# Gated branch products of a hybrid attention layer as seven half-size products each, and one expert's weights issued earlier

## The chip, the cores and the metric

One core of one Trainium2 chip. The metric is the device time of one execution, in microseconds (us); lower is better. All arithmetic of the part that is changed is float32.

## The reference, cut to what matters

One layer works on 256 tokens of width 1024. An input projection feeds two branches, differential attention (`y_a`) and a gated delta net (`y_b`), each 512 wide. They are merged by two gates, and a mixture of 32 experts follows:

```python
merged = (jax.nn.sigmoid(m_gate_a) * (y_a @ w_branch_attn[layer])
          + jax.nn.sigmoid(m_gate_b) * (y_b @ w_branch_gdn[layer]))
x = x + merged @ w_out[layer]
h2 = rms_norm(x, norm_ffn_gain[layer])
x = x + hier_moe(h2, ...)          # 32 experts, 1024 -> 256 -> 1024, two of them chosen per token
return rms_norm(x, norm_final_gain)
```

The change is in the two products `y @ w_branch`, each (256 x 512) by (512 x 1024).

## The kernel before

Five engine programs run side by side and meet at semaphores: `sync_program` issues nearly all transfers in one fixed order, `gpsimd_program`, `scalar_program`, `tensor_program` and `vector_program` compute. Work is laid out transposed: features on the 128 partitions, 256 tokens in the free direction.

**Stages.** The input projection is cut into 11 chunks of columns (`CHUNKS`, so `NCH` = 11) whose weights (2 MB each) alternate between two staging tiles, `stage0` and `stage1`. The last four chunks (`ma0`, `ma1`, `mb0`, `mb1`, the gates) are already computed with seven products of half size (`products`, L1022, matmul at L1046): GpSimd forms the four sums of weight quarters `S1`, `S2`, `S4`, `S3` (`combine` in `gpsimd_program`, L542, four instructions of 128x256 a form), ScalarE copies products `P1`, `P5`, `P6`, `P4` out of PSUM (L673), VectorE adds `P2`, `P3`, `P7` (L1892 to L1902), and ScalarE takes the sigmoid (L679). Then come the branch products (L1280 to L1301, matmul L1299): weights `w_branch_gdn` in `stage1`, `w_branch_attn` in `stage0`, four pieces `n` of 16 matmuls, each 128x128 weights on 256 token columns, written to a pair of PSUM banks. VectorE multiplies each piece with its gate (L2068) and adds the two branches to `merged` (L2071). Then `mix` (L1315) multiplies `merged` with `w_out`, whose halves use `stage1` and `stage0` again; `logits` (L1324), norms and routing follow, and then the loop over 32 experts (L1451 gate and up, L1494 down).

**A matmul of float32 counts twice** in the profile: the 64 matmuls of the branch products are 128 PE rows, and so on.

**What orders the transfers.** `sync_program` runs down one list and waits where a tile is not free. `stage_free(i)` (L335) waits until the stage tile of chunk `i` has been used. An expert's weights are three transfers of 1 MB (`load_expert`, L360 to L371), in eight slots. Slot 3 is the part of the arena from `A` to `EwT`; the gate and up weights of slot 7 lie in the tile `extra`, which holds the attention's exponentials before; slots 4 and 5 are `dv` to `vn` and `stage1`, slot 6 is `stage0`. Expert 5 waits for half of the mixing, expert 6 for all of it (`mix_out`, L366, L368). Later loads (L437, L442) wait until an expert has been used. The order around the change is: `w_branch_gdn` (L400), `w_branch_attn` (L400), expert 2, first half of `w_out` (L407), expert 3 and gate and up of slot 7, second half of `w_out`, experts 4, 5, 6.

Of the kernel before, what the change touches and what calls it, by code (L numbers as in the profile page):

```python
# [18 lines left out]
ALU = mybir.AluOpType  # L19
# [3 lines left out]
P = 128  # L23
# [5 lines left out]
H = 4  # L29
# [42 lines left out]
COPIED = ("P1", "P5", "P6", "P4")  # L72
ADDED = ("C11", "C12", "C2")
# [6 lines left out]
BANKS = {"ma0": (2, 0, 3, 1), "ma1": (0, 3, 2, 1), "mb0": (3, 2, 0, 1), "mb1": (1, 2, 0, 3)}  # L80
# [52 lines left out]
def lay_out(nc, ctx):  # L133
# [20 lines left out]
    def at(name, size, extra=0):  # L154
        return arena[:, names[name] + extra:names[name] + extra + size]
# [10 lines left out]
    def v3(ap, a):  # L166
        return ap.rearrange("p (a b) -> p a b", a=a)
# [55 lines left out]

    c.x1T = v3(at("qT", 2048), KD)
# [78 lines left out]
    def sem(name):  # L303
# [182 lines left out]
def gpsimd_program(pool, c, io):  # L486
# [96 lines left out]
def scalar_program(act, c, io):  # L583
# [347 lines left out]
def tensor_program(pe, c, io):  # L931
# [348 lines left out]
    for n in range(4):  # L1280
        j, half = n // 2, n % 2
        i = NCH + j
        w = c.stage[i % 2][:, 0:4096].rearrange("p (k n) -> p k n", k=H)
        yT = (c.ybT, c.yaT)[j]
        if n == 1:
            pe.wait_ge(s["ya_ready"], 1)
            turn("yaT", lambda i: c.oa[:, i % 2, (i // 2) * P:(i // 2 + 1) * P])
        pe.wait_ge(s[f"stage_loaded{i % 2}"], 16 * (i // 2 + 1))
        pe.wait_ge(s["ybT_ready" if j == 0 else "yaT_ready"], 1)
        if n == 0:  # L1290
            pe.wait_ge(s["product_copied"], copied("mb1", "P4"))
            pe.wait_ge(s["quarter_added"], added("mb1", "C11"))
        elif n == 1:
            pe.wait_ge(s["quarter_added"], added("mb1", "C2"))
        else:
            pe.wait_ge(s["branch_used"], n - 1)
# [4 lines left out]
        last.then_inc(s["branch_ready"], 1)  # L1301
# [356 lines left out]
def vector_program(v, c, io):  # L1658
# [745 lines left out]
```

## Time and profile before

| | us |
|---|---|
| median of 3 runs (453.85 to 455.72) | 455.1 |
| the profiled execution, its own time | 452.95 |
| its span, first to last instruction | 451.2 |
| PE busy | 422.8 (94%) |
| VectorE busy | 216.1 (48%) |
| ScalarE busy | 124.6 (28%) |
| GpSimd busy | 60.1 (13%) |
| moved by DMA | 136.92 MB, mean 303 GB/s |

Engines: PE is TensorE's matmuls, PEld its weight loads, DVE VectorE, ACT ScalarE, POOL GpSimd; SPq, PEq and so on are the sequencers that issue. The time of the profiled execution is 1.75 us more than its span. A busy share is a mean over stages that have different limits, so it doesn't tell what sets the time of a stage.

### The profile page before, as it was taken

Reading aid. Unit: us, or ns where it says so; the run is one execution under the profiler, and the core shown is the slowest. Engines: PE = TensorE matmul, PEld = TensorE weight load, DVE = VectorE, ACT = ScalarE, POOL = GpSimd, SP = SyncE. Lnnn points to the kernel's source line nnn. Section 1 sums busy time; section 2 is a strip of 40 time slices with the busy share of each in tenths; the row PEclk is TensorE's granted clock in tenths of the full one; section 3 lists DMA queues with packets and bytes.
Section 4 is the critical chain, followed back from the end, with each engine's and each line's share of the span. In section 5 each row is a group of like instructions: output and inputs, shape, how many; then the busy total and the mean of one; then the engine's idle time right before and its main releaser. Section 6 shows DMA issues by size and latency. Waiting matters only on the chain.

```text
span 451.2 us, 10749 instructions
## 1 busy us (share of the span) xinstructions
PE 422.8 (94%) x4503; PEld 337.8 (75%) x4503; DVE 216.1 (48%) x573; ACT 124.6 (28%) x326; POOL 60.1 (13%) x94
## 2 busy tenths in 40 slices
PE   9999999999999999999999899999999986779674
PEld 8885598884899999988889677777686755547351
DVE  3376777896446478022322654444453612433124
ACT  6001622100410455200012533233242411222144
POOL 4010600000558956000000000000000000000001
PEclk9999999999999999999999899999999998899899
DMA  8979826234805045389995999999999999999993
GB/s 308 409 243 302 288 80 214 96 120 100 321 2 188 16 171 187 125 348 410 404 421 201 380 390 425 414 422 420 422 425 418 420 426 420 421 424 421 420 398 118
DMA packets 38197, 136.92 MB, mean 303 GB/s; under 512 B 8592, under 2 KB 9936, under 8 KB 26256
## 3 DMA queue, kind: packets, MB, share of 16 engines
q1 hardware_dynamic: 33808, 135.22, 76.0%
q10 hardware_dynamic: 4352, 1.21, 1.2%
q8 instruction: 23, 0.38, 0.3%
q14 instruction: 14, 0.11, 0.1%
HBM read 134.59 MB, written 1.84 MB: 302 GB/s over the span
## 4 chain that ended last, share of the span: by engine, by line
PE 77%; DMA 18%; DVE 2%; ACT 1%; issue 1%; SPq 1%; POOLq 0%; ACTq 0%; DVEq 0%
PE ps L1000 22%; DMA arena<-in_moe_w_up 12%; PE ps L1046 11%; PE ps L1451 10%; PE ps L1315 6%; PE ps L1299 6%; DMA ring<-in_moe_w_up 6%; PE ps L1494 3%; PE ps L1504 3%; PE ps L1410 3%; PE ps L1459 1%; PE ps L1061 1%; PE ps L948 1%; PE ps L1399 1%; SPq L437 1%
## 5 line engine op out<-in xcount | busy, mean ns | idle before, releaser
L1000 PE MATMUL ps<-arena 128*128 128x256 f32 (+1 forms) x384 | 98.6, 416 | 0.0
L1000 PEld LDWEIGHTS ps<-arena 128*128 128x128 f32 x384 | 72.2, 190 | 22.3 <-issue 13.8
L1451 PE MATMUL ps<-arena 128*32 128x128 f32 x1040 | 38.3, 284 | 11.1 <-DMA arena<-in_moe_w_up 9.2
L1451 PEld LDWEIGHTS ps<-arena 128*32 128x32 f32 x1040 | 29.7, 110 | 17.8 <-DMA arena<-in_moe_w_up 8.4
L797 ACT ACTIVATE gains<-ps 32x256 f32<-32x256 f32 x62 | 23.4, 377 | 54.7 <-PE ps L1494 54.3
L563 POOL TENSOR_SCALAR ring<-ring,small 128x512 f32<-128x512 f32 x1 | 1.6, 1570 | 266.7 <-DVE small L2152 266.7
L2198 DVE TENSOR_TENSOR masks<-ps,masks 128x64 f32<-128x64 f32 x32 | 7.2, 224 | 54.8 <-ACT masks L778 54.6
L542 POOL TENSOR_TENSOR ring<-arena 128x256 f32<-128x256 f32 x32 | 22.7, 741 | 78.2 <-DMA arena<-in_w_in 65.7
L2214 DVE COPY arena<-ps 32x256 f32<-32x256 f32 x62 | 25.8, 416 | 11.4 <-PE ps L1494 10.5
L1451 PE MATMUL ps<-ring,arena 128*32 128x128 f32 x768 | 27.7, 285 | 3.3 <-DMA ring<-in_moe_w_up 3.3
L1315 PE MATMUL ps<-arena 128*128 128x256 f32 x128 | 29.3, 383 | 0.0
L1299 PE MATMUL ps<-arena 128*128 128x256 f32 x128 | 28.0, 379 | 0.0
L1410 PE MATMUL ps<-masks,arena 128*128 128x128 f32 x224 | 27.4, 281 | 0.0
L1451 PEld LDWEIGHTS ps<-ring,arena 128*32 128x32 f32 x768 | 22.1, 112 | 7.1 <-issue 4.0
L1410 PEld LDWEIGHTS ps<-masks,arena 128*128 128x128 f32 x224 | 26.0, 195 | 1.6 <-issue 1.6
L1299 PEld LDWEIGHTS ps<-arena 128*128 128x128 f32 x128 | 24.2, 190 | 3.2
L1315 PEld LDWEIGHTS ps<-arena 128*128 128x128 f32 x128 | 23.9, 190 | 3.0
L1046 PE MATMUL ps<-ring 128*128 128x128 f32 x192 | 23.1, 276 | 0.0
L1046 PEld LDWEIGHTS ps<-ring 128*128 128x128 f32 x192 | 22.1, 192 | 0.1
L1494 PE MATMUL ps<-arena,masks 128*32 128x256 f32 x304 | 20.1, 382 | 0.4 <-DMA arena<-in_moe_w_down 0.4
L739 ACT ACTIVATE arena<-arena 128x256 f32<-128x256 f32 x8 | 3.3, 416 | 46.0 <-DVE arena L2083 46.0
L784 ACT ACTIVATE masks<-ps 64x64 f32<-64x64 f32 x32 | 7.0, 217 | 32.6 <-PE ps L1459 32.6
(323 smaller groups left out, 606.5 us busy)
## 6 DMA issues: line engine op xcount, KB each, us to landing
arena<-in_moe_w_down SPq DMA_DIRECT2D x19, 1024.0 KB, 26.4
arena<-in_w_in SPq DMA_DIRECT2D x8, 2048.0 KB, 8.5
arena<-in_moe_w_gate SPq DMA_DIRECT2D x16, 1024.0 KB, 22.5
arena<-in_moe_w_up SPq DMA_DIRECT2D x16, 1024.0 KB, 23.5
ring<-in_moe_w_gate SPq DMA_DIRECT2D x12, 1024.0 KB, 20.1
ring<-in_moe_w_up SPq DMA_DIRECT2D x12, 1024.0 KB, 20.4
ring<-in_moe_w_down SPq DMA_DIRECT2D x12, 1024.0 KB, 21.7
arena<-in_w_out SPq DMA_DIRECT2D x2, 2048.0 KB, 10.4
```

The source lines that it names most:

```text
L542: pool.tensor_tensor(form[out][:, k, :], one[:, k, :], other[:, k, :], op).then_inc(s["forms_combined"], 1)
L797: last = act.activation(stacked(c, i, q), down_out(c, i, q), ACT.Copy)
L1000: last = pe.matmul(out, lhs, rhs, start=(k == 0 and (i > 0 or part % 2 == 0)), stop=(k == KD - 1), skip_group_check=(i == 0))
L1046: last = pe.matmul(out[:, a, :], forms[held][:, k, a * P:(a + 1) * P], forms[streamed][:, k, :], start=(begins and a == 0 and k == 0), sto ...
L1299: last = pe.matmul(blk(branch_out(c, half), b, TOK), w[:, k, (4 * half + b) * P:(4 * half + b + 1) * P], yT[:, k, :], start=(k == 0), stop ...
L1315: last = pe.matmul(mix_out(c, b), w[:, k, (b % 4) * P:(b % 4 + 1) * P], c.merged[k // 4][:, (k % 4) * TOK:(k % 4 + 1) * TOK], start=(k == ...
L1410: last = pe.matmul(gather_out(c, k), c.h2[:, t, k, :], c.oh[:, t, :], start=(t == 0), stop=(t == NT - 1))
L1451: last = pe.matmul(c.ps[ROWS * q:ROWS * (q + 1), i % 2, 0:P], c.Hg[:, k, ROWS * i:ROWS * (i + 1)], w[:, :, start:start + 127:2], start=(k ...
L1494: last = pe.matmul(down_out(c, i, q), c.actT[i % 2][:, kk * ROWS:(kk + 1) * ROWS], c.down_w[slot][:, kk, 256 * q:256 * (q + 1)], start=(kk ...
L1504: last = pe.matmul(y_out(c, half, t), c.S_e[:, t * P:(t + 1) * P], c.Y[half], start=False, stop=False, skip_group_check=True)
L2198: v.tensor_tensor(sg, bank[:, 0:64], sg, ALU.mult).then_inc(s["gated"], 1)
L2214: last = v.tensor_copy(stacked(c, i, q), down_out(c, i, q))
```

## The change

Each branch product is cut into quarters and computed as seven products of 8 matmuls with 128 token columns. GpSimd forms four sums of weight quarters a branch, VectorE four differences of `y` quarters (`form_branch`), ScalarE copies four products out (`copy_branch`), and VectorE adds the other three and applies the gates in smaller pieces. The transposition of `y_a` (`turn("yaT")`) is now in the middle of the first branch. On the list of transfers, expert 3 moves ahead of `w_branch_attn`, and gate and up of slot 7 move behind expert 4. The two halves of `w_out` wait for the seventh and the fourteenth product. Three blocks of `mix` instead of two are computed in halves before the first `logits`. `FORMS`, `BANK_OF` and `ORDER` are those of the gates.

```diff
+BRANCHES = ("b0", "b1")
+ALL_SEVEN = SEVEN + BRANCHES
-BANKS = {"ma0": (2, 0, 3, 1), "ma1": (0, 3, 2, 1), "mb0": (3, 2, 0, 1), "mb1": (1, 2, 0, 3)}
+BANKS = {"ma0": (2, 0, 3, 1), "ma1": (0, 3, 2, 1), "mb0": (3, 2, 0, 1), "mb1": (1, 2, 0, 3), "b0": (3, 2, 0, 1), "b1": (1, 2, 0, 3)}
...
+    c.branch_sum = {n: v3(at(place_, 1024), 2) for n, place_ in zip(COMBINED, ("dv", "cq", "kdec", "vn"))}
+    c.branch_form = [{n: v3(at("hT", TOK, 1024 * j + TOK * i), 2) for i, n in enumerate(("T1", "T3", "T2", "T4"))} for j in range(2)]
...
+    c.branch_part = [c.extra[:, 2048 * j:2048 * j + 2048].rearrange("p (a f) -> p a f", a=KD) for j in range(2)]
...
-            sp.wait_ge(s["branch_ready"], 2 * (i - NCH - 1))
+            sp.wait_ge(s["branch_ready"], len(ORDER) * (i - NCH - 1))
...
+        if j == 1:
+            sp.wait_ge(s["ybT_ready"], 1)
+            sp.wait_ge(s["ya_ready"], 1)
+            load_expert(3)
         stage_free(i)
         sp.dma_start(c.stage[i % 2][:, 0:4096].rearrange("p (k n) -> p k n", k=H),
...
-        if j == 0:
-            sp.wait_ge(s["ybT_ready"], 1)
-            sp.wait_ge(s["ya_ready"], 1)
-            load_expert(3)
-            load_expert(SLOTS - 1)
     sp.wait_ge(s["yaT_ready"], 1)
     sp.wait_ge(s["side_ready"], len(SIDE))
     sp.wait_ge(s["merged_ready"], 2)
     load_expert(4)
+    load_expert(SLOTS - 1)
...
+    for j, name in enumerate(BRANCHES):
+        i = NCH + j
+        w = branch_quarters(c, j)
+        def free(product):
+            if j:
+                pool.wait_ge(s["branch_ready"], branch_done(0, product))
+        def combine(out, one, other, op):
+            for k in range(2):
+                for f in range(2):
+                    cols = slice(TOK * f, TOK * f + TOK)
+                    pool.tensor_tensor(c.branch_sum[out][:, k, cols], one[:, k, cols], other[:, k, cols], op).then_inc(s["forms_combined"], 1)
+        pool.wait_ge(s[f"stage_loaded{i % 2}"], 16 * (i // 2 + 1))
...
+        free("P5")
+        combine("S1", w["A21"], w["A22"], ALU.add)
...
+        free("P6")
+        combine("S2", c.branch_sum["S1"], w["A11"], ALU.subtract)
...
+        free("P3")
+        combine("S4", w["A12"], c.branch_sum["S2"], ALU.subtract)
+        free("P7")
+        combine("S3", w["A11"], w["A21"], ALU.subtract)
...
+    copy_branch(0, "P1", "C11")
+    copy_branch(0, "P5", "C22")
+    copy_branch(0, "P6", "C12")
     act.wait_ge(s["side_ready"], SI["yaT"] + 1)
     act.activation(c.flat["qT"], c.side[side_pair("yaT")], ACT.Copy).then_inc(s["yaT_ready"], 1)
+    copy_branch(0, "P4", "C21")
...
-        for b in range(4):
-            for k in range(H):
-                last = pe.matmul(blk(branch_out(c, half), b, TOK), w[:, k, (4 * half + b) * P:(4 * half + b + 1) * P], yT[:, k, :],
-                                 start=(k == 0), stop=(k == H - 1))
...
+            out = branch_out(c, j, product)
+            for a in range(4):
+                for k in range(2):
+                    last = pe.matmul(out[:, a, :], forms[held][:, k, a * P:(a + 1) * P], forms[streamed][:, k, :],
+                                     start=(begins and a == 0 and k == 0), stop=(k == 1), skip_group_check=True)
+            last.then_inc(s["branch_ready"], 1)
+    branch_products(0, "P1", "P2", "P5", "P6")
+    pe.wait_ge(s["ya_ready"], 1)
+    turn("yaT", lambda i: c.oa[:, i % 2, (i // 2) * P:(i // 2 + 1) * P])
+    branch_products(0, "P4", "P3", "P7")
+    branch_products(1, "P1", "P2", "P5", "P6", "P4", "P3", "P7")
...
-        for b in range(2):
+        for b in range(3):
             mix(b, ks)
     logits(0)
-    for b in range(2, KD):
+    logits(1)
+    for b in range(3, KD):
...
-    for q in range(4):
-        v.wait_ge(s["branch_ready"], q + 1)
-        v.tensor_tensor(c.branch_gate[q], c.branch_gate[q], branch_out(c, q % 2), ALU.mult).then_inc(s["branch_used"], 1)
-        if q >= 2:
-            v.wait_ge(s["branch_used"], q + 1)
-            v.tensor_tensor(c.merged[q - 2], c.branch_gate[q - 2], c.branch_gate[q], ALU.add).then_inc(s["merged_ready"], 1)
+    form_branch(0)
+    add_branch(0, "C11", "P2", "P1")
+    add_branch(0, "C12", "P3", "P6")
...
+    chain(v.tensor_tensor(g0, g0, flat_half(0, 0), ALU.mult))
+    form_branch(1)
...
+    v.tensor_tensor(low, low, both_tokens(0), ALU.add).then_inc(s["quarter_added"], 1)
...
+    chain(v.tensor_tensor(g1, g1, flat_half(0, 1), ALU.mult))
+    add_branch(1, "C11", "P2", "P1")
...
+    chain(v.tensor_tensor(tokens(g2, 0), tokens(g2, 0), branch_part(c, 1, "C11"), ALU.mult))
...
+    chain(v.tensor_tensor(tokens(g2, 0), tokens(g2, 0), tokens(g0, 0), ALU.add))
+    v.wait_ge(s["product_copied"], copied("b1", "P6"))
+    early = branch_part(c, 1, "C12")
+    chain(v.tensor_tensor(early, early, tokens(g2, 1), ALU.mult))
...
+    chain(v.tensor_tensor(early, early, tokens(g0, 1), ALU.add))
+    v.wait_ge(s["product_copied"], copied("b1", "P4"))
+    low = flat_half(1, 1)
+    chain(v.tensor_tensor(low, low, g3, ALU.mult))
+    v.wait_ge(s["branch_ready"], branch_done(1, "P3"))
+    v.tensor_tensor(tokens(g2, 1), tokens(g2, 1), branch_out(c, 1, "P3"), ALU.mult).then_inc(s["quarter_added"], 1)
...
+    v.tensor_tensor(tokens(g2, 1), tokens(g2, 1), early, ALU.add).then_inc(s["merged_ready"], 1)
+    chain(v.tensor_tensor(low, low, g1, ALU.add))
...
+    v.tensor_tensor(gate3, gate3, both_tokens(1), ALU.mult).then_inc(s["quarter_added"], 1)
...
+    v.tensor_tensor(c.merged[1], low, g3, ALU.add).then_inc(s["merged_ready"], 1)
```

## Rows read from the trace of the kernel before

**Rows 1.** The chain that ended last, in order: start us, us, what

```profile
177.51 8.93 PE ps L1046 x80
186.44 6.91 PE ps L1299 x32
193.35 0.87 PE ps L1054 x8
194.22 20.72 PE ps L1299 x96
214.94 6.91 PE ps L1315 x32
...
335.74 26.11 DMA arena<-in_moe_w_up
```

**Rows 2.** Windows of busy time; the last three columns are PEclk, DMA share, GB/s

```profile
179.00:182.00 3.00, 3.00 (x29) 3.00 (x28) 1.03 (x4) 0.77 (x2) 0.00 (x0) 1.00 0.00 0
182.00:188.00 6.00, 6.00 (x48) 5.80 (x48) 1.11 (x2) 2.47 (x3) 0.00 (x0) 1.00 0.08 20
188.00:201.00 13.00, 13.00 (x66) 11.50 (x65) 1.22 (x1) 1.28 (x2) 0.00 (x0) 1.00 0.97 394
...
203.00:241.00 38.00, 38.00 (x188) 33.71 (x187) 9.89 (x25) 2.50 (x6) 0.00 (x0) 1.00 1.02 411
241.00:246.00 5.00, 5.00 (x31) 4.56 (x30) 1.27 (x3) 2.16 (x4) 0.00 (x0) 1.00 0.04 15
...
332.00:440.00 108.00, 88.94 (x1485) 62.40 (x1487) 37.00 (x114) 29.50 (x102) 0.00 (x0) 0.95 1.01 419
```

**Rows 3.** Timeline, SyncE's issues: start us, us, engine, line

```profile
171.30 0.37 SPq L400 DMA_DIRECT2D arena<-in_w_branch_gdn  x1
...
186.47 0.37 SPq L400 DMA_DIRECT2D arena<-in_w_branch_attn  x1
...
201.16 0.38 SPq L407 DMA_DIRECT2D arena<-in_w_out  x1
...
229.68 0.33 SPq L371 DMA_DIRECT2D arena<-in_moe_w_gate  x1
...
245.28 0.33 SPq L371 DMA_DIRECT2D arena<-in_moe_w_gate  x1
```

**Rows 4.** L400, the two branch weights: from issue to landing

```profile
DMA to landing us min/median/max: 7.7/7.8/7.9
```

**Rows 5.** Timeline around the start of the branch products

```profile
184.49 1.95 PE L1046 MATMUL ps<-ring 128*128 128x128 f32 x16
184.69 0.42 DVE L1896 TENSOR_TENSOR arena<-arena,ps 128x256 f32<-128x256 f32 x1 [4.66 <-PE ps L1046]
186.28 7.07 PE L1299 MATMUL ps<-arena 128*128 128x256 f32 x32
186.48 0.69 DVE L1902 TENSOR_TENSOR arena<-arena,ps 128x512 f32<-128x512 f32 x1 [1.36 <-PE ps L1046]
187.20 1.06 ACT L679 ACTIVATE arena<-arena 128x1024 f32<-128x1024 f32 x1 [2.61 <-DVE arena L1902]
...
214.78 7.07 PE L1315 MATMUL ps<-arena 128*128 128x256 f32 x32
```

**Rows 6.** Groups by line and shape: busy us, mean ns; one ScalarE copy of 128x512

```profile
L2088 DVE TENSOR_TENSOR arena<-arena 128x256 f32<-128x256 f32 x6 | 2.6, 426 | 2.9 <-ACT arena L739 2.9
L2071 DVE TENSOR_TENSOR arena<-arena 128x1024 f32<-128x1024 f32 x2 | 2.5, 1225 | 0.1
...
443.40 0.60 ACT L833 ACTIVATE ring<-ps 128x512 f32<-128x512 f32 x1 [0.17 <-PE ps L1480]
```

**Rows 7.** Timeline of GpSimd's sums, three forms in a row

```profile
136.88 2.79 POOL L542 TENSOR_TENSOR ring<-arena 128x256 f32<-128x256 f32 x4 [7.08 <-DVE extra L1929]
139.74 2.80 POOL L542 TENSOR_TENSOR ring<-ring,arena 128x256 f32<-128x256 f32 x4
142.62 2.79 POOL L542 TENSOR_TENSOR ring<-arena,ring 128x256 f32<-128x256 f32 x4
```

**Rows 8.** Single instructions of VectorE and GpSimd where both read SBUF

```profile
127.80 0.73 DVE L1998 TENSOR_TENSOR arena<-arena 128x512 f32<-128x512 f32 x1 [0.26 <-DVE arena L1994]
127.94 1.17 POOL L542 TENSOR_TENSOR ring<-arena 128x256 f32<-128x256 f32 x1
...
169.12 0.35 DVE L2046 SCALAR_TENSOR_TENSOR arena<-arena,small 128x128 f32<-128x128 f32 x1 [0.16 <-DVE arena L1937]
169.27 0.79 POOL L542 TENSOR_TENSOR ring<-ring,arena 128x256 f32<-128x256 f32 x1
169.39 0.81 DVE L2046 SCALAR_TENSOR_TENSOR arena<-arena,small 128x128 f32<-128x128 f32 x1
```

**Rows 9.** L2057 and L542 by line: ns min/median/max, first and last start

```profile
L2057 DVE SCALAR_TENSOR_TENSOR arena<-arena,small,gains x8: 336/339/915, 177.3 to 179.7; 128x128 f32<-128x128 f32 x8
...
L542 POOL TENSOR_TENSOR ring<-arena x32: 718/727/1172, 118.1 to 177.3; 128x256 f32<-128x256 f32 x32
```

**Rows 10.** Windows around TensorE's pause after the mixing, columns as before

```profile
248.00:250.00 2.00, 1.09 (x9) 0.79 (x7) 1.79 (x13) 2.00 (x2) 0.00 (x0) 1.00 1.03 434
...
252.00:254.00 2.00, 2.00 (x18) 0.65 (x17) 1.30 (x8) 0.00 (x0) 0.00 (x0) 0.50 1.04 438
```

More of the change, by code:

```diff
@@ L117, in copied, with branch_done, branch_formed @@
 def copied(name, product):
-    return len(COPIED) * SEVEN.index(name) + COPIED.index(product) + 1
+    return len(COPIED) * ALL_SEVEN.index(name) + COPIED.index(product) + 1
 def added(name, quarter):
-    return len(ADDED) * SEVEN.index(name) + ADDED.index(quarter) + 1
+    return len(ADDED) * ALL_SEVEN.index(name) + ADDED.index(quarter) + 1
 def combined(name, form):
-    return 4 + 4 * (len(COMBINED) * SEVEN.index(name) + COMBINED.index(form) + 1)
+    return 4 + 4 * (len(COMBINED) * ALL_SEVEN.index(name) + COMBINED.index(form) + 1)
+def branch_done(j, product):
+    return len(ORDER) * j + ORDER.index(product) + 1
+def branch_formed(j, form):
+    return 4 * j + ("T1", "T3", "T2", "T4").index(form) + 1
 class Core:
@@ L221, in lay_out @@
             c.form[f"B{i + 1}{j + 1}"] = c.hT[:, 4 * i:4 * i + 4, P * j:P * j + P]
+    c.branch_sum = {n: v3(at(place_, 1024), 2) for n, place_ in zip(COMBINED, ("dv", "cq", "kdec", "vn"))}
+    c.branch_form = [{n: v3(at("hT", TOK, 1024 * j + TOK * i), 2) for i, n in enumerate(("T1", "T3", "T2", "T4"))} for j in range(2)]
+    for j, yT in enumerate((c.ybT, c.yaT)):
+        for i in range(2):
+            for t in range(2):
+                c.branch_form[j][f"B{i + 1}{t + 1}"] = yT[:, 2 * i:2 * i + 2, P * t:P * t + P]
+    c.branch_part = [c.extra[:, 2048 * j:2048 * j + 2048].rearrange("p (a f) -> p a f", a=KD) for j in range(2)]
     c.x1T = v3(at("qT", 2048), KD)
@@ L569, in weight_quarters, with branch_quarters, branch_part, branch_out @@
     return {f"A{a + 1}{j + 1}": w[:, 4 * j:4 * j + 4, TOK * a:TOK * a + TOK] for a in range(2) for j in range(2)}
+def branch_quarters(c, j):
+    w = c.stage[(NCH + j) % 2][:, 0:4096].rearrange("p (k n) -> p k n", k=H)
+    return {f"A{a + 1}{k + 1}": w[:, 2 * k:2 * k + 2, 512 * a:512 * a + 512] for a in range(2) for k in range(2)}
+def branch_part(c, j, quarter):
+    a, t = int(quarter[1]) - 1, int(quarter[2]) - 1
+    return c.branch_part[j][:, 4 * a:4 * a + 4, P * t:P * t + P]
+def branch_out(c, j, product):
+    return c.ps[:, BANKS[BRANCHES[j]][BANK_OF[product]], :].rearrange("p (a f) -> p a f", a=4)
 def quarters(c, name):
@@ L1277, in tensor_program, with branch_free @@
     products("mb1", "P5", "P6", "P4", "P3", "P7")
-    for n in range(4):
-        j, half = n // 2, n % 2
-        i = NCH + j
[L1283 to L1287, printed above, removed]
+    def branch_free(name, product):
+        prev = ALL_SEVEN[ALL_SEVEN.index(name) - 1]
+        bank, was = BANKS[name][BANK_OF[product]], BANKS[prev]
+        if bank == was[3]:
+            pe.wait_ge(s["product_copied"], copied(prev, "P4"))
+        else:
+            pe.wait_ge(s["quarter_added"], added(prev, ("C2", "C11", "C12")[was.index(bank)]))
@@ L1288, in tensor_program, with branch_products @@
+    def branch_products(j, *wanted):
+        name = BRANCHES[j]
+        i = NCH + j
+        forms = dict(c.branch_form[j], **branch_quarters(c, j), **c.branch_sum)
         pe.wait_ge(s[f"stage_loaded{i % 2}"], 16 * (i // 2 + 1))
         pe.wait_ge(s["ybT_ready" if j == 0 else "yaT_ready"], 1)
[L1290 to L1296, printed above, removed]
@@ L1297, in tensor_program @@
-        for b in range(4):
-            for k in range(H):
-                last = pe.matmul(blk(branch_out(c, half), b, TOK), w[:, k, (4 * half + b) * P:(4 * half + b + 1) * P], yT[:, k, :],
-                                 start=(k == 0), stop=(k == H - 1))
-        last.then_inc(s["branch_ready"], 1)
+        for product in wanted:
+            held, streamed = FORMS[product]
+            begins = product in ("P1", "P2", "P5", "P4")
+            if begins:
+                branch_free(name, product)
+            if product == "P6":
+                pe.wait_ge(s["product_copied"], copied(name, "P1"))
+            elif product == "P3":
+                pe.wait_ge(s["product_copied"], copied(name, "P5"))
+            elif product == "P7":
+                pe.wait_ge(s["product_copied"], copied(name, "P6"))
+            if held in COMBINED:
+                pe.wait_ge(s["forms_combined"], combined(name, held))
+            if streamed[0] == "T":
+                pe.wait_ge(s["branch_forms"], branch_formed(j, streamed))
+            out = branch_out(c, j, product)
[4 more added lines that the diff above has]
+            last.then_inc(s["branch_ready"], 1)
@@ new lines, in both_tokens, with tokens, flat_half, add_branch @@
+    def both_tokens(j):
+        return branch_out(c, j, "P7").rearrange("p a (j f) -> p a j f", j=1).to_broadcast([P, 4, 2, P])
+    def tokens(flat, t):
+        return flat.rearrange("p (a f) -> p a f", a=4)[:, :, P * t:P * t + P]
+    def flat_half(j, half):
+        return c.extra[:, 2048 * j + 1024 * half:2048 * j + 1024 * half + 1024]
+    def add_branch(j, quarter, product, copy):
+        part = branch_part(c, j, quarter)
+        v.wait_ge(s["branch_ready"], branch_done(j, product))
+        v.wait_ge(s["product_copied"], copied(BRANCHES[j], copy))
+        v.tensor_tensor(part, part, branch_out(c, j, product), ALU.add).then_inc(s["quarter_added"], 1)
```

41 lines of the change are left out of this document (38 added, 3 removed).

## The prediction

> **What bounds the kernel now.** I read four views, in this order. First the chain that ended last [rows 1]. Up to some 332 us it is TensorE's own work without a gap: the gate products (L1046), the branch products (L1299), `mix` (L1315). From 335.74 us it is transfers of expert weights, 26 us at a time. The reader is to see that the end is set by DMA, and the stage with the change by TensorE. Second, the windows [rows 2]: from 332 to 440 us DMA is busy all the time at 419 GB/s. So a gain on TensorE counts only if it lets the last stretch of transfers start earlier. Third, that is the question of where DMA has run dry: it moves nothing from 179 to 182 us, next to nothing until 188, and 15 GB/s from 241 to 246. That second gap ends with the issue of expert 6 at 245.28 us [rows 3], which waits for the last block of `mix`, since its slot is `stage0`. What is moved after it has a fixed size. So the end moves with the end of `mix`, us for us, as long as DMA runs dry before it. Fourth, the timeline and the durations of single instructions give the prices [rows 5 to 9].
>
> **TensorE.** Before, from the first branch matmul at 186.28 to the first of `mix` at 214.78 us it takes 28.50 us [rows 5]: 128 rows of 256 columns and the transposition of 0.87 (6.91 + 20.72 = 27.63 for 128, 0.216 each [rows 1]). After, there are 14 products of 8 matmuls, which is 224 rows of 128 columns. That shape is L1046: 80 rows take 8.93 us, so 0.1116 each, 1.786 a product [rows 1]. 14 x 1.786 = 25.0; 27.6 - 25.0 = 2.6 us less. A seventh less arithmetic is 12.5% of 27.6 = 3.4; the shorter rows give 0.8 of it back. If nothing waits, `mix` starts at 212.2 instead of 214.8. `mix` has as many matmuls as before; that three blocks are begun in halves instead of two gives 5.2 us (24 rows of 0.216) instead of 3.5 until `merged[1]` is needed.
>
> **The transfers.** Expert 3 is issued when `ya_ready` comes, with the last L2057 at 180.0 us [rows 9], into the gap of DMA. 3.15 MB at 419 GB/s are 7.5 us, with the 1.9 us that pass between an issue at 186.47 and DMA's first data at about 188.4 [rows 2, 3]: 182.0 to 189.5. `w_branch_attn` is issued at 186.4 as before (it waits for `mb1`) and has 1.1 us of expert 3 ahead of it. Before, it landed 7.7 us after its issue, at 194.2 [rows 3, 4]; now I take 195.3. Behind it go expert 2, until 202, then `w_out`'s first half, issued after the seventh product at 199.7 instead of 201.16, until 207; `mix` wants it at 212. Then DMA is idle until `w_out`'s second half at 212.3 (before 214.97), which is wanted 14 us later. Expert 4 and slot 7 follow: 7.35 MB with it, 17.5 us, until 232. Expert 5 and expert 6 wait for `mix`, 229.68 and 245.28 before [rows 3]: expert 5 is issued near 227 and ends near 239, and expert 6 can't go before 242.7. DMA runs dry again, for 3 to 5 us, so this part gives and costs nothing by itself. The moved loads are paid for by idle time on both sides.
>
> **ScalarE** gets eight copies of 128x512, 0.60 each [rows 6]. It is free after the last sigmoid (187.20 + 1.06 [rows 5]). Each copy begins 0.2 after its product (as L1896 does in rows 5) and is wanted a whole product later, so it hides behind TensorE; without that cover each would cost 0.8.
>
> **GpSimd** gets 32 sums, four a form, 2.86 a form from start to start, 11.4 a branch [rows 7]. Branch 0: 179.3 (weights issued at 171.3 [rows 3], landed 7.9 later [rows 4]) to 190.6. TensorE wants the forms at 189.9, 191.6, 196.1 and 197.9, and they are there at 182.2, 185.0, 187.9 and 190.6. Branch 1: 195.3 to 206.7, wanted at 203.1, 204.9, 208.5 (`P3`) and 210.3 (`P7`), there at 198.2, 201.0, 203.9 and 206.7. 3.5 us of cover, so nothing, if GpSimd works at this pace.
>
> **VectorE is where it gets tight.** `mix` wants `merged[0]`, and its last inputs are late. Undisturbed, from rows 5 and 6 (0.43 for 256 columns, 0.68 for 512, 1.22 for 1024, 0.03 between): add `P3` of branch 0 at 198.0, gate 1.22, four forms 1.7, add `P7` 1.22, gate 1.22, add `P2` 0.68, multiply and add 1.36: at 206.5 it is done and waits for the copy of `P6` (207.6). Two instructions to 209.0, it waits for the copy of `P4` (209.4), multiplies 1024 columns to 210.6, then `P3`'s part and the last add: `merged[0]` at 212.0. TensorE comes at 212.2. No stall, but no slack either, and 1.6 us of waiting on VectorE's side. `merged[1]` comes at 215.8 and is wanted at 217.4.
>
> **But the two engines block each other.** The DVE instruction at 169.39 took 0.81 instead of 0.34 behind a GpSimd sum begun at 169.27, and the slowest L2057 took 0.915 against a median of 0.339; the GpSimd sum begun at 127.94, just after a DVE instruction with both inputs in SBUF, took 1.17 instead of 0.73 [rows 8, 9]. The one begun at 169.12 lost nothing. So a VectorE instruction with two SBUF inputs that meets GpSimd's sums pays 0, 0.47 or 0.58; I take 0.35 as a mean. In branch 1 eight such instructions fall between 198.7 and 209: the gate, four forms, the two with `g2`'s first tokens, the first with `early` (the second gate mostly meets a change of form). 8 x 0.35 = 2.8, less the 1.6 of waiting: `merged[0]` at 213.2 to 213.3. TensorE then stalls 1.2 before `mix`. GpSimd in turn loses 0.18 to a form, 0.45 to 512 columns [rows 8], and about 1.0 (0.45 and the 0.53 that 512 columns more take) to the gate: some 3 us, its last form at 209.5 to 210, wanted at 210.3. `merged[1]`: 217.0, wanted at 218.5.
>
> Beside the rows stands the Trainium skill, SBUF — State Buffer, section "Who interferes with whom": a VectorE instruction with two SBUF inputs and a GpSimd instruction that reads SBUF take an exclusive lock on a shared port, one waits for the other. The trace agrees in kind. The page holds the lock for the whole instruction; by that each meeting would cost up to 0.7, `merged[0]` would come near 215 and the gain would be nil. In rows 8 a sum gives way about 0.2 before its end, so I keep the rows' price.
>
> **The sum.** -2.6 (TensorE) + 1.3 (stall before `mix`, from `merged[0]` at 213.3 and 0.1 to TensorE, less rounding) = -1.3 us. The profiled execution would go from 452.95 to 451.65 us (span 451.2 to 449.9). It was 2.15 below the median of the runs shown, so on that median: 455.1 - 1.3 = 453.8 us. Bounds: the stall 0 (gain 2.6) to 2.9 (loss 0.3), if all eight pay 0.58.
>
> **The rivals.**
>
> *No blocking that matters (chance 0.25).* The meetings fall into gaps, as the first of 169.12 did. Then 2.6 less: 452.5. For it: only four meetings stand in rows 8 and 9, and 1.6 us of slack takes up the first four or five. Against: in branch 1 GpSimd has no pause.
>
> *VectorE pays in full (0.12).* Eight meetings of 0.5 to 0.58, gain between 0.4 and -0.3: 455.
>
> *GpSimd's sums late (0.13), the case on the slower side.* If `w_branch_attn` lands later, because expert 3 stands before it or shares with it, every form is late, and forms that are late meet more of VectorE's work. Up to a landing at 196 the chain above holds. From there on TensorE waits at `P5` to `P7`, and the waits of both engines add. Landing at 197, the last form would be 1.7 later than 209.8, at 211.5, and the two instructions with `early` and part of the next then meet it too (0.45, 0.45 and some 0.5): 212.9, 2.6 after it is wanted, and the gain is gone. Every us beyond costs a us and its share of such meetings, 1.5 together: at 198.5 it is slower by 2.3, 457.4. For it: expert 3 is 3.15 MB in front of a load that has 4 us of slack. Against: 1.1 us is all that is left of it at the issue, and landing times of rows 4 differ by 0.2.
>
> *The earlier load pays by itself (0.03).* 6.3 us of idle DMA from 182 to 188 are filled. If DMA didn't run dry before expert 6, the end would come up to 6 earlier: 449. Against it: 15 GB/s from 241 to 246 [rows 2].
>
> *The clock falls (0.05).* After TensorE's pause at 248 to 250 (1.09 of 2 us busy) the granted clock is 0.50 at 252 to 254 [rows 10], the lower level of 1.2 GHz. If the stall of 1.2 us did that to 4 us of `mix`, 2 us would be added: 455.8. Against: in rows 2 the clock stays at 1.00 everywhere up to 246.
>
> **How the numbers follow.** Forecast 0.42, the rivals 0.25, 0.12, 0.13, 0.03, 0.05. The likeliest time is 453.8, its own range 453.0 to 454.6. The bound of what a measurement can tell, 0.5%, is 2.3 us. Rival one, 2.6, lies just beyond and is measured as faster about half the time, and so is a tail of the forecast: faster 0.13 + 0.07 + 0.03 + 0.02 = 0.25. Slower is the late landing beyond 198 and half of the clock's case, with a tail: 0.13. Same 0.62. The range from 452.0 to 456.2 holds the forecast, rival one and two, and the milder half of the late landing.
>
> **What would show it.** The branch stage: 224 rows of 0.112, no idle before `P5` to `P7` (right), or waits for GpSimd there (rival three). `mix` starts at 213.5 (forecast), 212.2 (rival one) or 215. VectorE's two-input instructions at 0.7 to 0.9 instead of 0.43 for 256 columns, GpSimd's sums with a maximum over 1.2. Expert 6 issued at 244.0. DMA dry before it. The forecast is wrong if `mix` starts on time, or if the end doesn't follow the issue of expert 6.

## The result, and the profile after

| | before | changed |
|---|---|---|
| median, us | 454.4 (453.68 to 455.72, 8 runs) | 457.35 (455.08 to 458.73, 8 runs) |
| profiled execution: own time, span, us | 452.95, 451.2 | 455.08, 453.0 |
| first matmul of `mix`, us | 214.78 | 216.38 |
| issue of expert 6, us | 245.28 | 246.88 |

The ratio is 1.0059, with an interval from 1.0039 to 1.008: slower by 0.6%, some 2.7 us. Forecast were 453.8 us and a range up to 456.2. The forecast stood on 455.1, the median of the first three runs of the kernel before; as a change it was -1.3 us, on the 454.4 of eight runs 453.1.

The windows of the changed kernel. The columns are those of [rows 2]; of the last three, PEclk is the granted clock.

```profile
184.00:188.00 4.00, 4.00 (x38) 4.00 (x37) 1.75 (x3) 1.39 (x2) 3.92 (x7) 1.00 1.00 422
212.00:214.00 2.00, 0.00 (x0) 0.00 (x0) 1.90 (x3) 0.00 (x0) 2.00 (x3) 1.00 0.00 0
...
244.00:246.00 2.00, 2.00 (x11) 1.77 (x10) 0.32 (x1) 1.36 (x2) 0.00 (x0) 1.00 0.03 4
332.00:440.00 108.00, 90.30 (x1481) 63.23 (x1480) 36.85 (x113) 29.00 (x100) 0.00 (x0) 0.92 1.01 420
```

The frame of the forecast stands. The idle stretch of DMA before 188 us is filled (422 GB/s from 184 on), DMA is dry again before expert 6 (4 GB/s), and the last 108 us are transfers at 420 GB/s, as in [rows 2]. Expert 6 is issued 1.60 us later than before, exactly as much later as `mix` starts. What is new is the second row: TensorE does nothing from 212 to 214 us, while GpSimd and VectorE work. The chain that ended last shows how it came about (start us, us, what):

```profile
186.63 5.37 PE ps L1390 x48
...
192.05 5.83 issue
...
197.91 3.94 POOL arena L590 x4
...
201.93 3.23 POOL arena L590 x4
...
205.23 4.58 POOL arena L590 x4
...
209.95 2.02 PE ps L1390 x16
211.97 2.54 issue
214.52 2.02 PE ps L1390 x16
```

In [rows 1] this stretch was TensorE alone. Now the chain leaves it at 192 us, goes through a wait of 5.83 us on GpSimd's side and then through GpSimd's sums (L590): 3.2 to 4.6 us a form, where the forecast had 2.86. The timeline tells what GpSimd waited for. First the start of the chain of causes, VectorE's normalisation (L2150, which was L2057 in [rows 9]), GpSimd's sums for the first branch, and SyncE's issues:

```profile
177.46 4.15 DVE L2150 SCALAR_TENSOR_TENSOR arena<-arena,small,gains 128x128 f32<-128x128 f32 x8
179.23 12.17 POOL L590 TENSOR_TENSOR arena<-arena 128x256 f32<-128x256 f32 x16 [1.01 <-DMA arena<-in_w_branch_gdn]
...
181.69 0.34 SPq L389 DMA_DIRECT2D arena<-in_moe_w_gate  x1
...
186.66 0.38 SPq L422 DMA_DIRECT2D arena<-in_w_branch_attn  x1
```

and its two ends by DMA issue (KB, us from issue to landing), expert 3's last third and the branch weights behind it:

```profile
arena<-in_w_branch_attn SPq DMA_DIRECT2D x1, 2048.0 KB, 11.2
...
arena<-in_moe_w_down SPq DMA_DIRECT2D x1, 1024.0 KB, 10.2
```

Read them in order. The eight L2150 take 4.15 us, because GpSimd's sums begin in their midst at 179.23. So `ya_ready` comes at 181.6, expert 3 is issued at 181.69 instead of 180.1, and its last third lands 10.2 us after its issue at 182.54, at 192.8. The branch weights, 2.1 MB or 5.0 us at 419 GB/s, land behind it at 197.8, 11.2 us after their issue; before it was 7.7 [rows 4]. Then the second branch, again in the timeline:

```profile
197.91 16.51 POOL L590 TENSOR_TENSOR arena<-arena 128x256 f32<-128x256 f32 x16 [6.51 <-DMA arena<-in_w_branch_attn]
...
200.32 0.94 DVE L2162 TENSOR_TENSOR arena<-arena 128x256 f32<-128x256 f32 x1
...
206.90 1.19 DVE L2205 TENSOR_TENSOR arena<-arena,extra 128x512 f32<-128x512 f32 x1
...
211.41 1.74 DVE L2215 TENSOR_TENSOR extra<-extra,arena 128x1024 f32<-128x1024 f32 x1
...
213.85 1.12 DVE L2220 TENSOR_TENSOR arena<-arena,extra 128x512 f32<-128x512 f32 x1
...
209.95 2.02 PE L1390 MATMUL ps<-arena 128*128 128x128 f32 x16 [0.89 <-POOL arena L590]
214.52 2.02 PE L1390 MATMUL ps<-arena 128*128 128x128 f32 x16 [2.54 <-issue]
216.38 5.99 PE L1412 MATMUL ps<-arena 128*128 128x256 f32 x27
```

GpSimd starts at 197.91, and its 16 sums take 16.51 us instead of 11.4. VectorE's instructions on two SBUF inputs take 0.94 instead of 0.43 for 256 columns, 1.1 to 1.2 instead of 0.68 for 512, 1.74 instead of 1.22 for 1024. TensorE waits 0.89 before `P3` and 2.54 before `P7`. The second wait is put down to "issue", but the last sum ended at 214.42, 0.1 before `P7`. `merged[0]` (L2220) is there at 214.97, so even with `P7` in time `mix` could not have begun before 215.

### The profile page after: what moved, and what is told of

It reads as the page before. It is cut to its first block, busy times and chain, and to the rows that moved or that the text cites. A ratio compares the mean times of both kernels' runs of the same rounds, so it can differ in the third digit from the quotient of the medians.

```text
span 453.0 us, 11018 instructions
## 1 busy us (share of the span) xinstructions
PE 420.8 (93%) x4599; PEld 338.7 (75%) x4599; DVE 234.2 (52%) x591; ACT 129.4 (29%) x334; POOL 88.6 (20%) x126
## 4 chain that ended last, share of the span: by engine, by line
PE 72%; DMA 18%; POOL 3%; issue 2%; DVE 2%; ACT 1%; SPq 1%; POOLq 0%; ACTq 0%; DVEq 0%
PE ps L1076 21%; PE ps L1122 10%; PE ps L1549 10%; PE ps L1412 6%; DMA extra<-in_moe_w_up 6%; DMA arena<-in_moe_w_up 6%; DMA arena<-in_moe_w_down 5%; PE ps L1508 4%; PE ps L1592 4%; PE ps L1602 3%; POOL arena L590 3%; PE ps L1390 2%; PE ps L1557 1%; PE ps L1137 1%; DMA cst_in<-in_norm_ffn_gain 1%
## 5 line engine op out<-in xcount | busy, mean ns | idle before, releaser
L1549 PE MATMUL ps<-arena 128*32 128x128 f32 x1040 | 40.2, 298 | 9.7 <-DMA arena<-in_moe_w_up 9.6
L1549 PEld LDWEIGHTS ps<-arena 128*32 128x32 f32 x1040 | 31.2, 116 | 16.2 <-DMA arena<-in_moe_w_up 7.8
L2370 DVE COPY arena<-ps 32x256 f32<-32x256 f32 x62 | 25.8, 417 | 11.1 <-PE ps L1592 10.2
L590 POOL TENSOR_TENSOR arena<-arena 128x256 f32<-128x256 f32 x32 | 28.4, 920 | 7.8 <-DMA arena<-in_w_branch_attn 6.5
L1549 PE MATMUL ps<-ring,arena 128*32 128x128 f32 x768 | 26.5, 277 | 3.5 <-DMA ring<-in_moe_w_up 3.4
L1390 PE MATMUL ps<-arena 128*128 128x128 f32 x224 | 25.9, 276 | 3.4 <-issue 2.5
L1412 PE MATMUL ps<-arena 128*128 128x256 f32 x128 | 29.0, 382 | 0.0
L1549 PEld LDWEIGHTS ps<-ring,arena 128*32 128x32 f32 x768 | 21.1, 108 | 7.3 <-issue 3.9
```

Source lines behind the costliest of these rows:

```text
L590: pool.tensor_tensor(c.branch_sum[out][:, k, cols], one[:, k, cols], other[:, k, cols], op).then_inc(s["forms_combined"], 1)
L1390: last = pe.matmul(out[:, a, :], forms[held][:, k, a * P:(a + 1) * P], forms[streamed][:, k, :], start=(begins and a == 0 and k == 0), sto ...
L1412: last = pe.matmul(mix_out(c, b), w[:, k, (b % 4) * P:(b % 4 + 1) * P], c.merged[k // 4][:, (k % 4) * TOK:(k % 4 + 1) * TOK], start=(k == ...
L1549: last = pe.matmul(c.ps[ROWS * q:ROWS * (q + 1), i % 2, 0:P], c.Hg[:, k, ROWS * i:ROWS * (i + 1)], w[:, :, start:start + 127:2], start=(k ...
L2370: last = v.tensor_copy(stacked(c, i, q), down_out(c, i, q))
```

## The experiments

All on the chip, each compared with the kernel before in the same session (its median 454.2 to 454.4). "Start" is the first matmul of `mix` in the profiled execution, 216.38 in the changed kernel.

**First: is it the order of the loads or the products?** The changed kernel with expert 3 in its old place (gate and up of slot 7 stay behind expert 4):

```diff
-        if j == 1:
-            sp.wait_ge(s["ybT_ready"], 1)
-            sp.wait_ge(s["ya_ready"], 1)
-            load_expert(3)
         stage_free(i)
...
             .then_inc(s[f"stage_loaded{i % 2}"], 16)
+        if j == 0:
+            sp.wait_ge(s["ybT_ready"], 1)
+            sp.wait_ge(s["ya_ready"], 1)
+            load_expert(3)
     sp.wait_ge(s["yaT_ready"], 1)
```

> The seven products alone: expert 3 is issued behind the first half of the output weights again, the rest is the changed kernel (slot 7 stays behind expert 4, its tile is in use). Theory A (expert 3 ahead of the attention's branch weights makes GpSimd's sums late, and that is the whole loss): the weights land near 194.3 us instead of 197.8, the last sum ends near 210 instead of 214.4, no wait of TensorE before P7, mixing starts near 212.5, time 2 us under the kernel before. Theory B (GpSimd and VectorE blocking each other costs by itself, the order only adds): the weights land at 194.3 too, but VectorE's merged[0] is still late, mixing starts at 213.5 to 214.5, time 0.3 to 1.2 us under the kernel before.

Measured 452.63 (12 runs), ratio 0.9975 [0.9957, 0.9992], start 213.33. Its timeline:

```profile
194.60 18.03 PE L1390 MATMUL ps<-arena 128*128 128x128 f32 x160
...
194.48 14.30 POOL L590 TENSOR_TENSOR arena<-arena 128x256 f32<-128x256 f32 x16 [2.92 <-DMA arena<-in_w_branch_attn]
...
200.44 0.94 DVE L2162 TENSOR_TENSOR arena<-arena 128x256 f32<-128x256 f32 x1
...
209.25 0.68 DVE L2210 TENSOR_TENSOR extra<-extra,arena 128x512 f32<-128x512 f32 x1
...
212.49 0.69 DVE L2220 TENSOR_TENSOR arena<-arena,extra 128x512 f32<-128x512 f32 x1
...
213.33 4.99 PE L1412 MATMUL ps<-arena 128*128 128x256 f32 x22 [0.69 <-DVE arena L2220]
```

The weights land 7.6 us after their issue, the sums run from 194.48 to 208.8, and no product waits (160 matmuls in one piece). VectorE meets the sums just as often in the forms, but from 209 on its instructions are back at 0.68, and it delivers `merged[0]` at 213.18. TensorE waits 0.69 before `mix`. So without the early expert 3 the products do what the forecast's sum says, and expert 3 ahead of the branch weights costs 3.0 us of start. The loads of slot 7, which are still late here, aren't the cause.

**The order alone**, both moved loads, on the kernel before:

```diff
+        if j == 1:
+            sp.wait_ge(s["ybT_ready"], 1)
+            sp.wait_ge(s["ya_ready"], 1)
+            load_expert(3)
         stage_free(i)
...
-        if j == 0:
-            sp.wait_ge(s["ybT_ready"], 1)
-            sp.wait_ge(s["ya_ready"], 1)
-            load_expert(3)
-            load_expert(SLOTS - 1)
...
     load_expert(4)
+    load_expert(SLOTS - 1)
```

> The kernel before with the moved loads alone (expert 3 ahead of the attention's branch weights, slot 7 behind expert 4), products as before. Theories A and B: TensorE wants these weights only near 201 us and they land by 198, DMA runs dry before expert 6 in any case, so no change within 0.3 us of the kernel before. Theory C (the moved loads cost later, in the expert loop, whatever the products do): 1 to 2.5 us slower than the kernel before, with expert 6 issued at the same time.

454.14 (12 runs), 0.9994 [0.9975, 1.0012], start 215.15. Expert 3 is issued at 180.49 here and the branch weights land at 196.9, 10.0 us after their own issue and 2.3 later than before, and nobody minds: here TensorE alone waits for them, and it is busy with the first branch until then. So the products (with slot 7 late) give 0.25%, the moved loads nothing, and both together cost 0.6%. The loss is in what couples them: GpSimd, which needs the weights earlier than TensorE does.

**Is it the blocking or the lateness?** Two kernels keep the late weights. The first leaves out six of VectorE's instructions with two SBUF inputs:

```diff
-    chain(v.tensor_tensor(g0, g0, flat_half(0, 0), ALU.mult))
-    form_branch(1)
+    v.wait_ge(s["yaT_ready"], 1)
+    v.sem_inc(s["branch_forms"], 4)
...
-    chain(v.tensor_tensor(g1, g1, flat_half(0, 1), ALU.mult))
```

> The changed kernel without six of VectorE's instructions with two SBUF inputs between 199 and 206 us: the two multiplications of the first branch with its gates and the four differences for the second branch are left out (their results are wrong or stale). Theory B (port blocking): GpSimd's four sums of the second branch take 12 to 13.5 us instead of 16.5, though their weights still land at 197.8; TensorE waits under 1 us before P7; mixing starts at 212.2 to 213; 2 us under the kernel before. Theory A (late landing alone): the sums still end 16 us after the landing, mixing starts near 215.5, time at or above the kernel before.

453.14 (10 runs), 0.9982 [0.996, 1.0005], start 214.20. The sums take 14.02 instead of 16.51 us, though the weights land at 198.15:

```profile
198.22 14.02 POOL L590 TENSOR_TENSOR arena<-arena 128x256 f32<-128x256 f32 x16 [6.82 <-PE ps L1390]
...
212.34 2.02 PE L1390 MATMUL ps<-arena 128*128 128x128 f32 x16 [1.62 <-issue]
214.20 8.15 PE L1412 MATMUL ps<-arena 128*128 128x256 f32 x37
```

That is less than the expectation for blocking had: 12 to 13.5 us of sums, a wait of TensorE under 1 us (it is 1.62) and a start up to 213. The six instructions are worth 2.5 us of sums and 2.2 of start; VectorE's later ones still meet GpSimd.

In the second GpSimd's sums of the second branch are half as wide, and half of each is left out:

```diff
-                    cols = slice(TOK * f, TOK * f + TOK)
+                    cols = slice(TOK * f, TOK * f + (P if j else TOK))
```

> The changed kernel with GpSimd's sixteen sums of the second branch on 128 columns instead of 256 (half of each sum is left out, the other half is stale). If GpSimd's lateness sets the start of mixing, it goes to 212.2 to 213.2 and the time to 1.5 to 2.5 us under the kernel before. If VectorE's chain to merged[0] sets it by its own length, mixing starts at 214 or later and the time is within 1 us of the kernel before.

452.11 (7 runs), 0.9951 [0.9926, 0.9976], start 212.45:

```profile
198.15 10.92 POOL L590 TENSOR_TENSOR arena<-arena 128x128 f32<-128x128 f32 x16 [6.68 <-DMA arena<-in_w_branch_attn]
...
194.53 18.03 PE L1390 MATMUL ps<-arena 128*128 128x128 f32 x160
212.45 9.74 PE L1412 MATMUL ps<-arena 128*128 128x256 f32 x44
...
200.43 0.68 DVE L2162 TENSOR_TENSOR arena<-arena 128x256 f32<-128x256 f32 x1
```

Here GpSimd has less work, so this run shows that the length of its stream sets the start, not by itself that blocking does. The blocking shows in the last line: beside sums of 128 columns, which take 0.45 alone, L2162 takes 0.68, beside sums of 256, which take 0.72, it takes 0.94, and alone 0.43. Half the width of GpSimd's instruction costs VectorE half as much, 0.25 instead of 0.51.

Both load late, at 198, as the changed kernel does. With sums that end at 209.1 no product waits, and `mix` starts within 0.3 of the 212.2 that TensorE's work alone gives. So it takes both: late weights, and sums that take 4 us a form. Early weights turn the loss into a gain; less blocking alone turns it into no change.

**A version to beat both.** The attention's branch weights go first, into the ring slot of expert 3, where they find DMA idle; expert 3 follows when they have been used. The second half of `w_out` goes into `stage0` as soon as the last gate chunk is done:

```diff
...
-            load_expert(3)
-        stage_free(i)
-        sp.dma_start(c.stage[i % 2][:, 0:4096].rearrange("p (k n) -> p k n", k=H),
+        sp.dma_start(branch_weights(c, j).rearrange("p (k n) -> p k n", k=H),
...
     sp.wait_ge(s["proj_ready"], parts_before(NCH))
...
+    load_out(1)
+    load_expert(OWN - 1)
+    sp.wait_ge(s["branch_ready"], len(ORDER))
+    load_out(0)
+    sp.wait_ge(s["branch_ready"], 2 * len(ORDER))
+    load_expert(3)
...
+def branch_weights(c, j):
+    return c.ring[3][:, 0:4096] if j else c.stage[NCH % 2][:, 0:4096]
```

> The seven products with another order of transfers: the attention's branch weights are issued at ya_ready into the place of slot 3 (free then), the second half of the output weights into stage0 as soon as mb1 is done, expert 3 only after the second branch. If the loss of the changed kernel is the late landing of these weights (run on the late sums of GpSimd), they land near 189.5 us, GpSimd goes on from branch to branch without the pause of 6.5 us and ends by 207, TensorE never waits in the products, and mixing starts at 212.2 to 213.3; time 1 to 2.5 us under the kernel before and at or below the version with the old order. If VectorE's chain is the limit whatever GpSimd does, mixing starts at 213.3 as in that version.

452.43 (9 runs) against 454.42, 0.9953 [0.9932, 0.9973], start 212.59. Issued at 181.94, the weights are there at 190.8:

```profile
192.33 5.63 POOL L594 TENSOR_TENSOR arena<-arena 128x256 f32<-128x256 f32 x8 [0.70 <-PE ps L1404]
198.56 8.36 POOL L594 TENSOR_TENSOR arena<-arena 128x256 f32<-128x256 f32 x8 [0.60 <-PE ps L1404]
...
206.96 0.69 DVE L2219 TENSOR_TENSOR arena<-arena,extra 128x512 f32<-128x512 f32 x1
...
212.59 9.73 PE L1426 MATMUL ps<-arena 128*128 128x256 f32 x44
```

The first two forms cost 5.63 us, at full pace, before VectorE's work of that branch begins; the other two take 8.36 against it; L2219 (L2205 above) is at 0.69 instead of 1.19. This is the lowest median here of a kernel that computes everything, 2.0 us below the kernel before; its interval overlaps that of the changed kernel with expert 3 in its old place (0.9957 to 0.9992), so the two can't be told apart. With the half-wide sums on top:

> The version with early attention weights, and GpSimd's sums of the second branch on 128 columns instead of 256 (half of each left out). If blocking by GpSimd costs this version nothing any more, mixing starts within 0.2 us of its 212.6 and the time is the same within the measurement. If blocking still costs, mixing starts up to 0.4 earlier.

451.81 (10 runs), 0.9947 [0.9923, 0.9972], start 212.43: nothing more that can be told apart. What is left of the blocking in that version costs 0.2 us of start by these two profiles.

**Does expert 2, right behind the branch weights, share their bandwidth?** The changed kernel with `load_expert(OWN - 1)` moved behind the first half of `w_out`:

```diff
-    sp.wait_ge(s["proj_ready"], parts_before(NCH))
-    load_expert(OWN - 1)
...
+        if j == 0:
+            load_expert(OWN - 1)
```

> The changed kernel with expert 2 issued behind the first half of the output weights instead of directly behind the attention's branch weights. If these weights land late (11.2 us after issue instead of 7.7) because expert 3 stands before them, nothing changes: landing 10.5 to 11.5 us after issue. If it is sharing with expert 2 that follows them in a queue that is already full, they land 8.5 to 9.5 us after issue, at 195.5, and mixing starts near 213.5 to 214.5, the time near the kernel before.

456.8 (7 runs), 1.0068 [1.003, 1.0106], start 216.31; the weights land at 197.7, 16.3 us after the issue of expert 3, as in the changed kernel (16.2). What follows them costs nothing; what stands before them is the cause. Its windows show one thing more, the last three rows a quarter of a us wide:

```profile
192.00:196.00 4.00, 4.00 (x38) 4.00 (x38) 0.00 (x0) 2.22 (x3) 0.00 (x0) 1.00 0.95 383
196.00:198.00 2.00, 2.00 (x20) 2.00 (x20) 0.00 (x0) 0.60 (x1) 0.25 (x1) 1.00 0.05 20
...
196.00:196.25 0.25, 0.25 (x4) 0.25 (x4) 0.00 (x0) 0.00 (x0) 0.00 (x0) 1.00 0.12 49
...
197.00:197.25 0.25, 0.25 (x4) 0.25 (x4) 0.00 (x0) 0.25 (x1) 0.00 (x0) 1.00 0.08 33
197.25:197.50 0.25, 0.25 (x5) 0.25 (x4) 0.00 (x0) 0.03 (x1) 0.00 (x0) 1.00 0.00 0
```

From 196 us on DMA moves next to nothing, and yet the landing is seen 1.7 us later. In between a share of 0.12 or less is busy, two of the 16 DMA engines at most, until 197.25. So most of the load is there, and a small part of it comes late.

**The changed kernel again, and its clock.** Unaltered, twice more; and the kernel before once more:

> The changed kernel unaltered, for a second profile. Theory D (what is missing between the start of mixing, 1.6 us later, and the medians, 2.7 to 2.9 us apart, lies in the routing stage, where the clock fell in one execution and not in the other): the time from the issue of expert 6 to the first reload is 12.0 or 13.1 us, as in the other runs, and the profiled time follows it. Theory E (the landing of the weights varies): mixing starts later than 216.4 by up to 1.3.

> The changed kernel unaltered, for a third profile; the same two theories as for the second one.

> The kernel before unaltered, for a second profile. Theory D: its time from the issue of expert 6 to the first reload is 12.0 or 13.1 us, in either case with the start of mixing at 214.8 to 215.2.

456.25 (10 runs), 1.0037 [1.0006, 1.0067], start 217.27; then one execution of 455.75 us, start 216.02; one of the kernel before, 453.5 us, start 215.05. The first of them shows something that the others don't, in its timeline and its windows:

```profile
210.21 2.02 PE L1390 MATMUL ps<-arena 128*128 128x128 f32 x16 [0.89 <-POOL arena L590]
214.78 2.71 PE L1390 MATMUL ps<-arena 128*128 128x128 f32 x16 [2.55 <-issue]
217.27 5.08 PE L1412 MATMUL ps<-arena 128*128 128x256 f32 x18
```

```profile
215.00:216.00 1.00, 1.00 (x11) 1.00 (x11) 1.00 (x2) 0.00 (x0) 0.00 (x0) 0.96 0.00 0
216.00:217.00 1.00, 1.00 (x7) 1.00 (x6) 0.36 (x1) 0.00 (x0) 0.00 (x0) 0.50 0.08 16
217.00:218.00 1.00, 1.00 (x5) 0.91 (x4) 0.48 (x1) 0.00 (x0) 0.00 (x0) 0.50 0.00 0
218.00:219.00 1.00, 1.00 (x4) 0.73 (x4) 0.90 (x2) 0.00 (x0) 0.00 (x0) 0.50 0.48 68
```

After the pauses of 0.89 and 2.55 us the granted clock is 0.50 (1.2 of 2.4 GHz) for 3 us, and `P7` takes 2.71 instead of 2.02. The other two profiles of the changed kernel show 1.00 there, after pauses of 0.89 and 2.54 us and of 0.20 and 2.99. So I filled both pauses with useless matmuls:

```diff
+            if j == 1 and product in ("P3", "P7"):
+                for _ in range(3 if product == "P3" else 11):
+                    pe.matmul(c.ps[:, 7, 0:P], c.ident, c.ident, start=True, stop=True)
```

> The changed kernel with 3 and 11 matmuls of 128x128 without use (0.22 us each) in TensorE's two pauses, ahead of its waits for GpSimd before P3 and P7 of the second branch; nothing else changes. If part of the median's rise is the clock that falls after these pauses (granted 0.50 from 216 to 219 us in the second profile of the changed kernel, not in the first and third), the clock stays at 1.00 up to 248 us in every profile, mixing starts at 216.0 to 216.8, and the median is 0.5 to 1.5 us under the changed kernel's 456.3 to 457.4, still over the kernel before. If the clock has no part in it, the median stays at 457 or rises.

455.57 (12 runs), 1.0028 [1.0006, 1.0049], start 216.18. TensorE no longer waits before `P3` and waits 0.43 before `P7`; the clock is at 1.00 until 252. One such profile tells nothing, since two of three without the filling show 1.00 too. The median is the lowest of the four sets of the same work (456.25, 456.8 and 457.35 the others), but the intervals overlap: it fits a clock that falls in some executions, and doesn't prove it.

## Why the prediction was wrong, by its own steps

**TensorE, right.** 160 matmuls in 18.03 us are 0.1127 each, against 0.1116. Where nothing waits, `mix` starts at 212.4 to 212.6 (forecast 212.2). One wording of the forecast is wrong and its number right: seven products for eight are an eighth less arithmetic, 12.5%, not a seventh.

**The end follows `mix`, right for the medians.** In each of the 13 profiles the span is 205.6 to 208.2 us longer than the time at which expert 6 is issued, and that issue comes 30.5 to 30.6 us after the start of `mix` (31.5 where the clock fell in it). Each median is its kernel's start plus 238.9 to 239.8 us, but for the changed kernel's own 457.35 (241.0) and the one with expert 2 later (240.5). A single execution follows less closely: from the first reload of an expert slot to the end it takes 192.9 to 195.5 us in the 13 profiles, and no run here shows why.

**VectorE and the blocking, right in place and sum.** With the old order `merged[0]` came at 213.18, forecast 213.2 to 213.3, and GpSimd lost 14.30 - 11.4 = 2.9 us, forecast some 3. The single price was too low: not 0.35 as a mean with some at nothing, but 0.4 to 0.5 at each meeting of 256 or 512 columns (0.94 for 0.43, 1.19 for 0.68); against it, only six of the eight that I counted paid it, since the gate's cost 0.12 and the sums had ended by the last. 0.12 + 1.93 + 0.93 = 3.0, forecast 2.8. That the sum came out is in part luck: a price too low and a count too high. The Trainium skill, SBUF — State Buffer, section "Who interferes with whom", has one of the two wait for the other's lock; the trace agrees in kind, 0.94 for 0.43 us. By whole instructions it had been 215 for `merged[0]`; 213.18 was measured.

**The transfers, wrong: this is the step that failed.** The forecast put GpSimd's waits at nothing ("3.5 us of cover, so nothing, if GpSimd works at this pace"), and that cover hung on the time of landing; measured are waits of 0.89 and 2.54 us. "Expert 3 is issued when `ya_ready` comes, with the last L2057 at 180.0 us", "has 1.1 us of expert 3 ahead of it", "now I take 195.3". Measured 181.69 and 197.8. Of these 2.5 us, 1.6 come from the issue. I charged the blocking to the second branch and left it out of the first, where the forecast itself has the sums begin at 179.3, amid the eight L2057. By line, ns min/median/max, the L2057 of [rows 9] have become

```profile
L2150 DVE SCALAR_TENSOR_TENSOR arena<-arena,small,gains x8: 339/574/903, 177.5 to 180.8; 128x128 f32<-128x128 f32 x8
...
L590 POOL TENSOR_TENSOR arena<-arena x32: 722/776/1708, 179.2 to 213.7; 128x256 f32<-128x256 f32 x32
```

a median of 574 instead of 339, 4.15 instead of 2.75 us in all. The other 0.9 is in the queue: DMA moves 82 GB/s up to 184 and then 422, 400 and 404 in the three stretches of 4 us up to 196, in all 5.23 MB, what expert 3 and the branch weights have together; the landing is seen 1.8 us after that, where the forecast had 0.8. It is 1.7 without expert 2 behind it too, so that it isn't shared bandwidth. The trace has the landing of each load in 16 parts, and it is one part that is late: of the branch weights 15 are there by 197.02 and the last at 197.84; in the kernel before all 16 come between 193.72 and 194.20. Of expert 3 the first third has no such straggler (all there by 186.89), the second has one (190.26 after 189.34), the third again (192.78 after 191.95). Between the landings of the first third and the second falls a transfer of instructions, 16 KB in 1.0 us at 187.46, while DMA is busy; in the kernel before it comes at 184.34, into idle DMA. Queue 8 from 187 to 189 us in the changed kernel and from 184 to 186 in the one before:

```profile
q8 instruction: 1, 0.02, 3.1%
...
q8 instruction: 1, 0.02, 2.9%
```

It is so in all 13 profiles: in the three where this transfer comes at 184.3 to 184.6 the last part of the branch weights is 0.03 to 0.13 us behind the fifteenth, in the ten where it comes at 187.0 to 187.8, amid loads, it is 0.6 to 1.2 behind. That the instructions hold up one of the DMA engines is read from this order of events; no run tests it.

**So rival three held, nearly in its numbers.** It said: from a landing at 197 on "the gain is gone", and each further us costs 1.5. At 197.8 that gives a last form at 214.1 and a start 1.2 later than before; measured 214.4 and 1.6. It had a chance of 0.13 because I held against it that "landing times of rows 4 differ by 0.2": those were loads with nothing in front of them. The slack of 3.5 us between forms and products was counted undisturbed; after the 3 us that the same text lets GpSimd lose, 0.3 to 0.8 was left, and that is less than the 2.5 us by which the landing was off.

**The clock, rival five, in part.** A fall after the pauses is seen in one of three profiles of the changed kernel and costs it 0.7 in `P7` alone. It can explain why the median rises by 2.7 where the start moves by 1.0 to 2.5 (216.02 to 217.27, against 214.78 and 215.05); shown it is not, and the scatter of 2.6 us after the first reload is as large. A second scatter, of 1.1 us, has nothing to do with the change: from the issue of expert 6 to the first issue of the reloads it takes 12.0 us, or 13.1 to 13.4 where the clock falls in the routing. It did so in 3 of the 13 profiles, and one of them is the profile of before that I worked from [rows 10]: 13.06, but 11.97 in the second profile of the same kernel.

## What to carry to other kernels

Two parts of a change that are each harmless can meet in a third engine. Ask of every transfer that is moved who needs it first after the change, not who did before, and count the slack after the slowdowns you have already granted. Where VectorE and GpSimd both work on SBUF, charge each meeting to both engines and in every stretch where their streams overlap, above all where a semaphore hangs on the end of one of them. An idle stretch of DMA is best given to what is wanted next: here the seven products with the branch weights first are 0.5% faster than the kernel before, with expert 3 first 0.6% slower.

## What the runs showed of the hardware

- While GpSimd adds 128x256 fp32 in SBUF, a VectorE instruction with two SBUF inputs takes mostly 0.4 to 0.5 us more, at three widths (0.94 for 0.43, 1.19 for 0.68, 1.74 for 1.22; two of 1024 columns paid 0.12 and 0.01), and a sum up to 1.71 instead of 0.72. Beside sums of 128x128 it is 0.25 (0.68 for 0.43). With PSUM as one input it takes what it takes alone (L2217, 0.67).
- Three loads of 1 MB, issued together at 181.7 to 182.5 into an idle DMA, landed 5.2, 8.2 and 10.2 us after their issues, and a 2 MB load issued 5 us behind the first landed 11.2 us after its own: the queue was worked off nearly in order. From the second load on one of the 16 parts of each landed 0.8 to 0.9 us behind the others, after an instruction transfer of 16 KB at 187.46.
- Of three executions of the same program one had the granted clock at 0.50 for 3 us after pauses of 0.89 and 2.55 us; the other two, with pauses of 0.89 and 2.54 us and of 0.20 and 2.99, kept 1.00.
